# First projection of a two-block transformer kernel: x loaded already transposed on a second DMA queue, row factor moved behind the products, first two weight units run k-outer, small vectors packed

## The chip, the core and the metric

One core of one Trainium2 chip runs the whole program. The metric is the device time in microseconds (us), the median of the runs shown. The engines are TensorE (PE; PEld is its weight load), VectorE (DVE), ScalarE (ACT), GpSimd (POOL) and SyncE (SP, which here only issues DMAs). "SPq" and "ACTq" are the DMA queues of SP and ACT. Each engine runs its own instructions in program order and waits on semaphores.

## What is computed

Two transformer blocks on x of 512 tokens x 1024 features, in float32. Only the start of the first block matters here:

```python
h = rms_norm(x, norm_g)          # x * r * g,  r = rsqrt(mean(x*x) + eps), one r per token
proj = h @ w_in                  # 1024 x 3864
dq, dk, dv, dz, nq, nkv, nz, ng = jnp.split(proj, IN_SPLITS, axis=-1)
dq = rms_norm(dq per head of 64, diff_q_norm_g)     # dk, nq, k_slc, k_win alike
kc, vc = compress(nkv[0], ...), compress(nkv[1], ...)
```

After it come differential attention, the three branches of sparse attention (compressed, selected, window), an output projection, and a second block with a convolution, another attention and a feed-forward net.

## The kernel before, in words

**Split products.** Every float32 projection is made of three reduced-precision products: a weight piece `w_hi` (ACT copies `raw` into it), the rest `w_lo` (POOL subtracts), and likewise `h_hi` (ACT) and `h_lo` (DVE) for the activations. A 128x512 output tile takes 8 k-steps x 3 products = 24 matmuls.

**Units.** Weights come in units of 256 columns (1 MB, two tiles of 128 output features each), in the order dq 0-1, cmp (keys and values to be compressed), dk 0-1, dq 2-3, dk 2-3, nq 0-1, nq 2-3, kd (nsa keys), then the value units. `raw`, `w_hi` and `w_lo` have two slots, so unit n+2 takes the slot of unit n. SP issues the load of a unit when POOL has read the slot's `raw`; ACT splits `w_hi` of the next unit while PE works on this one.

**Plan.** One list of steps (`plan`) is written out beforehand; every engine walks it in the same order and executes its own part of each step. What an engine does for one step therefore stands in front of everything it does for later steps. `later(n, ...)` puts a step n slots on, where a slot is a run of four k-steps (12 matmuls) of PE.

**Head norm.** A tile of kind dq, dk, nq or kd is followed by: squares on ACT into a scratch tile of `L` (L1120 to L1123, read from PSUM), the head's sum of squares as a matmul with a block of ones on PE (`sums`, L1905, one step for the two tiles of a unit, placed after the first 12 matmuls of the next unit or after half of `hidden`), the square root on ACT (L1155, L1156), the reciprocal on DVE (L1460) and the multiplication on POOL (L1040). The tile itself is copied out of PSUM with its gain by DVE (L1401), after ACT's squares.

**cmp tiles.** DVE copies each into `shifted` (L1427, L1428, four copies) and builds `flat` from it (L1436, two additions); `hidden` multiplies that on PE (L2028).

**Start.** SP loads x (four pieces of 512 KB) and then the first unit; ACT's queue has an identity, norm_g and two small tables. ACT and DVE compute the row factor r, DVE scales x by it, PE transposes the scaled x (L1815), ACT and DVE make `h_hi` and `h_lo` from it (L1299, L1762). PE runs 22 idle matmuls first (L2081), and the small matmuls of the bias table (L2085). Twenty small DMAs bring the gain and bias vectors as rows; PE transposes them in one go (L2140), and DVE's `small_arrays` prepares what is derived from them (L1377 to L1393), among it `causal_distance` plus the mask, whose end is signalled as `setup_done` (L1389). The very first squares of a dq tile on ACT wait for `setup_done`.

The three lines that tie the first squares to that setup (two of ACT, one of DVE):

```python
if t.x_in == 1:
    sc.wait_ge(setup_done, 1)
v.tensor_tensor(causal_distance, causal_distance, mask, ALU.add).then_inc(setup_done, 1)
```

Of the kernel before, what the change touches and what calls it, by code (L numbers as in the profile page):

```python
# [9 lines left out]
P = 128  # L10
T = 512
# [21 lines left out]
LAG = 3  # L33
PIECE = 512
# [15 lines left out]
N_SMALL = 20  # L50
# [4 lines left out]
def shape_constants():  # L55
# [10 lines left out]
    steps += [np.full((P, 1), 4.0 ** (h + 1)) for h in range(DIFF_HEADS)]  # L66
    const = np.concatenate([np.eye(P), ones, mask, np.where(ok, 0.0, BIG).reshape(P, -1),
# [44 lines left out]
def build(nc, a, out):  # L112
# [65 lines left out]
    COL_BANK = 5  # L178
# [36 lines left out]
    hi_in_pieces = order[0], *beside_attention, out1_u[0], branch_u[0]  # L215
    ring_in, lo_pieces = [0, 0], Counter()
    for n, u in enumerate(order):
# [8 lines left out]
        ring_in[n % 2] += 16 * (len(u.parts) if u.parts else 1)  # L226
        u.arrived = ring_in[n % 2]
        u.act0 = down_u.index(u) if u.act else None
    next_of = {u.n: order[u.n + 1] if u.n + 1 < len(order) else None for u in order}
# [12 lines left out]
    def evacuated(t):  # L242

        if t.kind in NORM:
            ax_slot(t)
            t.x_in = upto("aux_in")
            t.ve = upto("ve_evac")
# [5 lines left out]
        elif t.kind in ("cmp", "kik", "z", "nz"):  # L253
            t.norms, t.auxes = count["norm_done"], count["aux_done"]
            t.sc = upto("sc_evac") if t.kind in ("z", "nz") else None
            t.ve = upto("ve_evac")
            left[t.bank] = [("ve_evac", t.ve)]
        elif t.kind == "hidden":
# [110 lines left out]
    norms_so_far = [0]  # L369
# [96 lines left out]
    for i in range(NT):  # L466
        emit("row", nth=0, half=1, i=i, res=0)
    left[COL_BANK] = [("col_done", 1)]
    left[4], left[0] = [("rows_done", 1)], [("rows_done", 2)]
    transposed_norm(R_NORM, (1, COL_BANK, 6, 7, 2, 3, 4))  # L470
    first_pieces = [0]

    def small_arrays():

        first_pieces[0] += 1
        if first_pieces[0] != 2:
            return
        col_waits, left[COL_BANK] = left[COL_BANK], [("col_done", 2)]
        emit("small_arrays", waits=col_waits)
# [19 lines left out]
    project(dq_u[:1] + [kv_u] + dk_u[:1], RING4, 4, small_arrays)  # L499
# [194 lines left out]
    with ctx:  # L694
# [10 lines left out]
        lam_in = sb("lam_in", [P, 4, DH])  # L705
# [17 lines left out]
        vec_rows = PT[0:NROWS, 0, 0:P]  # L723
# [20 lines left out]
        dq, dk, nq, dv, kd = (region(2048 * j, 4, T) for j in range(5))  # L744
        vd = region(10240, 2, NT, P)
# [57 lines left out]
        ST_CMN, ST_CSM, ST_TOP, ST_DSS, ST_C2, ST_DC, ST_GNQ, ST_GDQ = 100, 116, 132, 160, 256, 288, 216, 220  # L803
# [28 lines left out]
        def turned_free(t):  # L832

            if t in turned_before:
# [4 lines left out]
        const_in, w0_in = sem("const_in"), sem("w0_in")  # L839
        first_in, small_in, w1_in = sem("first_in"), sem("small_in"), [sem(f"w1_in{j}") for j in range(4)]  # L840
# [8 lines left out]
        col_tr, col_done, setup_done, eps_done = sem("col_tr"), sem("col_done"), sem("setup_done"), sem("eps_done")  # L849
        lam_dot, lam_exp, zero_done = sem("lam_dot"), sem("lam_exp"), sem("zero_done")  # L850

        second_square = sem("second_square")
# [41 lines left out]
                       h_hi_done=h_hi_done, col_done=col_done,  # L894
# [21 lines left out]
        def squares_at(nth, half, i):  # L916

            return max(i, 1) if nth == 0 else NT - 1 + 2 * NT * (nth - 1) + NT * half + i + 1

        def normed_at(nth, i):  # L920

            return (NT + 2) * nth + i + 1

        gains = dict(dq=lambda idx: st[:, ST_GDQ + idx:ST_GDQ + idx + 1], dk=lambda idx: col[:, R_GDK:R_GDK + 1],
                     nq=lambda idx: st[:, ST_GNQ + idx:ST_GNQ + idx + 1], kd=lambda idx: col[:, R_GKS + idx:R_GKS + idx + 1])
# [17 lines left out]
        def _(sp):  # L943
            def load(u):
                if u.n >= 2:
                    wait_free(sp, [(order[u.n - 2].lo_by, order[u.n - 2].lo_end)])
                if u.n == 0:
                    src, half = u.parts[0][0], u.nk // 2
# [6 lines left out]
            def small_loads():  # L955
# [10 lines left out]
                def small(dst, src):  # L966
                    nonlocal n_small
                    sp.dma_start(dst, src).then_inc(small_in, 16)
                    n_small += 1
# [1238 lines left out]
```

## Time and profile before

| what | value |
|---|---|
| median of 3 runs | 1061.03 us (1060.91 to 1061.03) |
| span of the profiled execution, first to last instruction | 1059.3 us |
| PE busy | 1049.8 us (99%) |
| DVE, ACT, POOL busy | 496.7, 455.8, 398.5 us |
| first matmul of the projection starts | 13.37 us |
| PE reaches `hidden` of the compressed keys (144 matmuls and one `sums` later) | 48.58 us |

Read it from PE: almost all of the span is its own work in a row. What another engine does costs time only where PE waits for it. The table gives the one profiled execution; what lies around its span up to the median is 1.7 us.

### The profile page before, as it was taken

The page shows a single profiled execution, that of the slowest core. Times are in us where ns is not written, and L with a number is a line of the kernel's source. Part 1 is how long each engine was busy: PE and PEld are TensorE (multiplying, and loading weights), DVE is VectorE, ACT ScalarE, POOL GpSimd, SP SyncE. Part 2 cuts the span into 40 slices and gives each one's busy share as a digit, 9 for nine tenths or more (in the row PEclk, how much of TensorE's full clock was granted, in tenths as well). Part 3 has the DMA queues.
Part 4 walks back from the last instruction along what each step waited for, and adds up shares of the span by engine and source line. Part 5 has one row for each costly group of instructions (what it writes and reads, how often), then busy time and mean ns, then how long its engine had stood idle before and what let it go on. Part 6 is the DMA issues. An engine that isn't in the chain of part 4 may idle for free.

```text
span 1059.3 us, 14497 instructions
## 1 busy us (share of the span) xinstructions
PE 1049.8 (99%) x5573; PEld 839.1 (79%) x5573; DVE 496.7 (47%) x1047; ACT 455.8 (43%) x794; POOL 398.5 (38%) x300
## 2 busy tenths in 40 slices
PE   9999999999999999999999999999999999999997
PEld 7777897767678876888777888888888888888886
DVE  5754688875752316998587344230000000032444
ACT  6455557676653425233465414342221221233533
POOL 3555520001025334446000255434435354465772
PEclk9999999999999999999999999999999999999999
DMA  9631221201032331332221232323232323323221
GB/s 296 189 117 54 71 80 41 76 16 47 25 120 80 72 118 41 102 98 80 80 80 41 80 103 96 90 79 110 82 116 79 115 83 103 115 80 100 82 97 80
DMA packets 84724, 95.72 MB, mean 90 GB/s; under 512 B 8121, under 2 KB 70930, under 8 KB 84666
## 3 DMA queue, kind: packets, MB, share of 16 engines
q1 hardware_dynamic: 83706, 92.46, 27.9%
q0 software_dynamic: 560, 2.12, 0.6%
q8 instruction: 38, 0.62, 0.2%
q10 hardware_dynamic: 400, 0.35, 0.1%
q14 instruction: 20, 0.16, 0.0%
HBM read 92.80 MB, written 2.12 MB: 90 GB/s over the span
## 4 chain that ended last, share of the span: by engine, by line
PE 97%; DVE 1%; DMA 1%; ACT 1%; issue 0%; ACTq 0%; DVEq 0%
PE bank L1864 59%; PE bank L2177 23%; PE bank L1923 4%; PE bank L1954 3%; PE bank L1995 3%; PE bank L1971 1%; PE bank L2152 1%; PE bank L1815 1%; PE bank L2028 1%; PE bank L1905 1%; DMA PT<-in_onehot 1%; PE bank L1984 0%; PE bank L1947 0%; PE bank L2073 0%; DVE L L1506 0%
## 5 line engine op out<-in xcount | busy, mean ns | idle before, releaser
L1030 POOL TENSOR_TENSOR w_lo<-raw,w_hi 128x512 fp32r<-128x512 f32 (+1 forms) x190 | 266.8, 1434 | 435.1 <-ACT w_hi L1092 422.6
L1864 PE MATMUL bank<-h_hi,w_hi 128*128 128x512 f32 (+1 forms) x560 | 224.4, 401 | 0.3 <-ACT h_hi L1299 0.2
L1864 PE MATMUL bank<-h_hi,w_lo 128*128 128x512 f32 (+1 forms) x560 | 218.7, 390 | 0.0
L1864 PE MATMUL bank<-h_lo,w_hi 128*128 128x512 f32 (+1 forms) x560 | 217.8, 390 | 0.0
L1092 ACT ACTIVATE w_hi<-raw 128x512 fp32r<-128x512 f32 (+3 forms) x94 | 111.3, 1214 | 118.1 <-PE bank L1864 114.5
L1070 POOL TENSOR_TENSOR w_lo<-raw,w_hi 128x512 fp32r<-128x512 f32 x88 | 110.7, 1290 | 133.5 <-ACT w_hi L1337 67.1
L1864 PE MATMUL bank<-w_hi,h_hi 128*128 128x512 f32 (+2 forms) x397 | 145.4, 366 | 0.0
L1864 PE MATMUL bank<-w_hi,h_lo 128*128 128x512 f32 (+2 forms) x397 | 144.5, 364 | 0.0
L1864 PE MATMUL bank<-w_lo,h_hi 128*128 128x512 f32 (+2 forms) x397 | 144.5, 364 | 0.0
L2177 PE MATMUL bank<-h_hi,w_hi 128*128 128x512 f32 x352 | 137.1, 389 | 0.0
L2177 PE MATMUL bank<-h_hi,w_lo 128*128 128x512 f32 x352 | 137.1, 389 | 0.0
L2177 PE MATMUL bank<-h_lo,w_hi 128*128 128x512 f32 x352 | 136.8, 389 | 0.0
L1864 PEld LDWEIGHTS bank<-h_hi,w_hi 128*128 128x128 f32 (+1 forms) x560 | 104.7, 187 | 30.8 <-issue 8.7
L1864 PEld LDWEIGHTS bank<-h_hi,w_lo 128*128 128x128 f32 (+1 forms) x560 | 104.7, 187 | 22.9
L1864 PEld LDWEIGHTS bank<-h_lo,w_hi 128*128 128x128 f32 (+1 forms) x560 | 104.9, 187 | 21.0 <-DVE h_lo L1762 0.4
L1800 DVE TENSOR_TENSOR pool<-bank,L 128x512 f32 (+1 forms) x22 | 15.2, 691 | 215.7 <-PE bank L2177 215.7
L1864 PEld LDWEIGHTS bank<-w_hi,h_hi 128*128 128x128 f32 x397 | 74.8, 188 | 14.5 <-issue 2.1
L1864 PEld LDWEIGHTS bank<-w_hi,h_lo 128*128 128x128 f32 x397 | 74.8, 188 | 11.8
L1864 PEld LDWEIGHTS bank<-w_lo,h_hi 128*128 128x128 f32 x397 | 74.8, 188 | 11.7
L2177 PEld LDWEIGHTS bank<-h_hi,w_hi 128*128 128x128 f32 x352 | 66.1, 188 | 13.9 <-ACT h_hi L1299 0.2
L2177 PEld LDWEIGHTS bank<-h_lo,w_hi 128*128 128x128 f32 x352 | 66.1, 188 | 13.8
L2177 PEld LDWEIGHTS bank<-h_hi,w_lo 128*128 128x128 f32 x352 | 66.1, 188 | 13.7
(211 smaller groups left out, 1240.4 us busy)
## 6 DMA issues: line engine op xcount, KB each, us to landing
raw<-in_w_in SPq DMA_DIRECT2D x29, 1024.0 KB, 5.3
raw<-in_w_ffn_gate SPq DMA_DIRECT2D x11, 1024.0 KB, 5.3
raw<-in_w_ffn_up SPq DMA_DIRECT2D x11, 1024.0 KB, 5.3
raw<-in_w_out SPq DMA_DIRECT2D x8, 1024.0 KB, 5.0
raw<-in_w_ffn_down SPq DMA_DIRECT2D x8, 1024.0 KB, 5.0
raw<-in_w_in SPq DMA_DIRECT2D x8, 512.0 KB, 4.5
pool<-in_cmp_w SPq DMA_DIRECT2D x4, 1024.0 KB, 9.1
raw<-in_w_ffn_down SPq DMA_DIRECT2D x4, 768.0 KB, 4.3
```

The source lines that it names most:

```text
L1030: nc.gpsimd.tensor_tensor(w_lo[:, u.n % 2, cols], raw[:, u.n % 2, cols], w_hi[:, u.n % 2, cols].bitcast(F32), ALU.subtract).then_inc(lo_do ...
L1070: nc.gpsimd.tensor_tensor(w_lo[:, n % 2, cols], raw[:, n % 2, cols], w_hi[:, n % 2, cols].bitcast(F32), ALU.subtract).then_inc(lo_done, 1)
L1092: act_fn(w_hi[:, u.n % 2, cols], raw[:, u.n % 2, cols], ACT.Copy).then_inc(hi_done, 1)
L1800: v.tensor_tensor(x, bank[2 + j][:, :], L[:, j, :], ALU.mult).then_inc(act_done, 1)
L1815: return nc.tensor.transpose(bank[t.bank][:, P * i:P * i + P], zs[:, i, P * t.idx:P * t.idx + P], ident)
L1864: ins = mm(bank[t.bank][0:t.m, 0:u.width if u.token else T], stationary, moving, start=first and n == 0, stop=last and n == len(products) ...
L1905: ins = mm(bank[banks[half]][o:o + DH, :], ones[rows, rows], scratch(t)[rows, :], start=True, stop=True)
L1923: ins = mm(bank[S_BANKS[c]][:, columns(job, p)], q, k, start=True, stop=True)
L1954: ins = nc.tensor.transpose(dst[:, o:o + P], L[:, (job.r + c) % LRING, o:o + P], ident)
L1971: ins = mm(O[:, P * p:P * p + P], turned(job.t)[:, o:o + P], dv[:, j, P * g:P * g + P], start=j == 0, stop=j == i)
L1995: ins = mm(O[DH * half:DH * half + DH, P * i:P * i + P], x, turned(job.t + half)[:, o:o + P], start=dsa and j == 0, stop=j == i and (dsa o ...
L2177: ins = mm(bank[2 * j + m][:, :], w[:, k, P * m:P * m + P], x[:, k, :], start=n == 0, stop=n == len(products) - 1)
```

## The change

- **x arrives transposed.** The host lays x out as `x_t` (feature by token); ACT's queue loads `cols` (all small vectors, already as columns) and then x_t in 8 pieces of 256 KB, then the two tables. SP's queue loads the first two units in 8 pieces of 256 KB, then the constants, the lambda vectors and `distance`. PE's transposes, their PSUM tiles and the 20 small DMAs are gone. x in its old layout (needed for the residual) is loaded after unit 6.
- **Row factor behind the products.** `h_hi` and `h_lo` are made from x_t times norm_g only. ACT squares x_t, DVE adds the squares up, PE multiplies by ones (`ss`), ACT takes the root and DVE the reciprocal, into `rbc` (r for every token, on all partitions). Each output tile of this block is multiplied by `rbc` when DVE takes it out of PSUM (dv and vd tiles: by a column on ACT).
- **Head norm.** DVE now takes the tile out first (times `rbc`); ACT squares the copy in SBUF; for dk and kd tiles ACT then also multiplies it by the gain in place. q gains are folded into the k gains.
- **nz and z tiles.** DVE takes the tile out, ACT makes tanh of the copy, and DVE finishes it one slot later (`z_finish`): one more DVE instruction per tile, 8 tiles.
- **k-outer head.** The first two units run together: for each k, 4 tiles x 3 products, with waits on each piece. The third unit's `w_hi` is split in four pieces as the head frees them.
- **Places.** `small_arrays` and the bias-table matmuls stand behind the head, in the third unit.

The pieces of the diff, in this order: the plan; ACT's head; ACT's squares of a tile; DVE taking tiles out (norm tiles, then cmp tiles); the loads on ACT's queue.

```diff
-    project(dq_u[:1] + [kv_u] + dk_u[:1], RING4, 4, small_arrays)
+    emit("head")
+    emit("split", u=order[2], of=order[1])
+    for o in range(0, PIECE * len(head_part), PIECE):
+        emit("high_piece", u=order[2], o=o)
+    for t in head_tiles[:2]:
+        evacuated(t)
+    emit("high_piece", u=order[2], o=PIECE * len(head_part))
+    for t in head_tiles[2:]:
+        evacuated(t)
+    for u in head_units:
+        follow(u)
+    project(dk_u[:1], RING4, 4, small_arrays)
...
+            def head():
+                for q in range(ND // 2):
+                    for k in (2 * q, 2 * q + 1):
+                        sc.wait_ge(xt_in[k], 16)
...
+                        act_fn(h_hi[:, k, :], x_t[:, k, :], ACT.Copy, scale=col[:, R_NORM + k:R_NORM + k + 1]).then_inc(h_hi_done, 1)
+                        for j in range(2) if k % 2 == 0 else ():
...
+                            act_fn(w_hi[:, j, cols], raw[:, j, cols], ACT.Copy).then_inc(hi_done, 1)
...
+                        act_fn(square_rows[:, k % 2, :], x_t[:, k, :], ACT.Square).then_inc(sq_done, 1)
+                sc.wait_ge(ss_mm, 1)
+                act_fn(rbc[:, :], bank[4][:, :], ACT.Sqrt, scale=1.0 / D, bias=eps).then_inc(r_root, 1)
...
-                sc.wait_ge(tile_done, t.done)
-                if kind in NORM + AUX_COPY:
+                if kind in NORM:
                     if t.x_in == 1:
                         sc.wait_ge(setup_done, 1)
+                    sc.wait_ge(ve_evac, t.ve)
...
+                    if t.squared:
+                        ins.then_inc(row_squares, 1)
+                        sc.wait_ge(row_squares, t.squared)
+                        ins = act_fn(x, x, ACT.Copy, scale=gains[kind](idx))
...
                 if kind in NORM:
-                    ve.wait_ge(aux_in, t.x_in)
+                    ve.wait_ge(tile_done, t.done)
...
+                    if kind in ("dq", "nq"):
+                        v.scalar_tensor_tensor(dests[kind][:, idx, :], src[:, :], steps_at(kind, idx), rbc[:, :],
+                                               ALU.mult, ALU.mult).then_inc(ve_evac, 1)
+                    else:
+                        v.tensor_tensor(dests[kind][:, idx, :], src[:, :], rbc[:, :], ALU.mult).then_inc(ve_evac, 1)
...
-                        v.tensor_copy(shifted[0:DH, idx, kv, :], src[half, :])
+                        v.tensor_tensor(shifted[0:DH, idx, kv, :], src[half, :], rbc[half, :], ALU.mult)
...
+            sc.dma_start(col[:, :], a["cols"]).then_inc(cols_in, 16)
+            for k in range(ND):
+                sc.dma_start(x_t[:, k, :], a["x_t"][:, k, :]).then_inc(xt_in[k], 16)
```

How instructions now stand, at three places.

On DVE, at the setup. `L1389` before and `L1456` after are the addition that signals `setup_done`; L1401 takes dq tiles out of PSUM before, L1516 ends the second cmp tile after. Before:

```order
L1381 TENSOR_SCALAR st<-const,col 128x4 x2
L1383 TENSOR_SCALAR col<-col 128x16
L1384 TENSOR_SCALAR col<-col 128x1
L1386 ISA lam_in,st<-lam_in 128x64
L1386 ISA st 128x1
L1386 ISA lam_in,st<-lam_in 128x64
L1386 ISA st 128x1
L1389 TENSOR_TENSOR pool<-pool,const 128x512
L1391 TENSOR_TENSOR st<-st 128x1
L1393 TENSOR_SCALAR st<-st 128x1
L1401 TENSOR_SCALAR pool<-bank,st 128x512 x2
```

After:

```order
L1516 TENSOR_TENSOR zs<-zs,col 128x496 x2
L1448 TENSOR_SCALAR col<-col 128x1
L1449 TENSOR_SCALAR col<-col 128x3
L1450 TENSOR_SCALAR col<-col 128x16
L1451 TENSOR_SCALAR col<-col 128x1
L1453 ISA pool,st<-pool 128x64
L1453 ISA st 128x1
L1453 ISA pool,st<-pool 128x64
L1453 ISA st 128x1
L1456 TENSOR_TENSOR pool<-pool,const 128x512
L1458 TENSOR_TENSOR st<-st 128x1
```

The setup stood ahead of every tile that DVE takes out; now it stands behind two dq tiles and both cmp tiles.

On ACT, from the last work of the first activations to the first squares (L1123, L1120, L1121 before; L1168, L1166 after) and the weight splits (L1092 before; L1130 after). Before:

```order
L1299 ACTIVATE h_hi<-bank,col 128x512 [waits tile_done] x2
L1092 ACTIVATE w_hi<-raw 128x2048 [waits raw_in1]
L1322 ACT_TABLE_LOAD
L1322 ACTIVATE st<-st 128x2 [waits lam_dot]
L1123 ACTIVATE L<-bank 128x512 [waits setup_done,tile_done]
L1120 ACTIVATE L<-bank 64x512 [waits tile_done]
L1121 ACTIVATE L<-bank 64x512
L1092 ACTIVATE w_hi<-raw 128x2048 [waits tile_done,raw_in0]
```

After:

```order
L1119 ACTIVATE rbc<-bank,st 128x512 [waits ss_mm]
L1120 ACTIVATE st<-bank,st 128x4
L1130 ACTIVATE w_hi<-raw 128x512 [waits part_done,raw_in0] x3
L1168 ACTIVATE L<-pool 128x512 [waits ve_evac,setup_done]
L1166 ACTIVATE L<-pool 64x512 [waits ve_evac]
L1166 ACTIVATE L<-pool 64x512
L1130 ACTIVATE w_hi<-raw 128x512 [waits tile_done,raw_in0]
L1130 ACTIVATE w_hi<-raw 128x2048 [waits tile_done,raw_in1]
```

The first squares wait for `setup_done` as before and now for DVE's copy too; the last piece of the third unit's `w_hi` and the whole fourth unit stand behind them.

On DVE, at the reciprocals (L1460 before, L1540 after) and the tiles taken out around them (L1401 before, L1476 and L1473 after); L1731 and L1804 copy `hidden`. Before:

```order
L1460 RECIPROCAL L<-L 128x512 x2
L1427 COPY zs<-bank 64x512
L1428 COPY zs<-bank 64x511
L1427 COPY zs<-bank 64x512
L1428 COPY zs<-bank 64x511
L1436 TENSOR_TENSOR zs<-zs,col 128x496 x2
L1401 TENSOR_SCALAR pool<-bank,col 128x512 x2
L1731 COPY pool<-bank 62x128 x2
```

After:

```order
L1464 TENSOR_SCALAR L<-bank 8x512
L1476 TENSOR_TENSOR pool<-bank,rbc 128x512
L1540 RECIPROCAL L<-L 128x512 x2
L1476 TENSOR_TENSOR pool<-bank,rbc 128x512
L1804 COPY pool<-bank 62x128 x2
L1473 SCALAR_TENSOR_TENSOR pool<-bank,const,rbc 128x512 x2
```

The second dk tile is taken out behind the two reciprocals of the dq tiles both times; but ACT's squares of that tile come ahead of it before, and from it after.

## Rows read from the trace of the kernel before

**Rows 1.** Page, part 1: busy time, share of the span, instructions of each engine.

```profile
PE 1049.8 (99%) x5573; PEld 839.1 (79%) x5573; DVE 496.7 (47%) x1047; ACT 455.8 (43%) x794; POOL 398.5 (38%) x300
```

**Rows 2.** Whom PE waited for, whole span: total us, times, longest us.

```profile
PE bank L2081 <- POOL vc L1042: 1.0, 1, 1.0
PE bank L2085 <- DMA PT<-in_onehot: 0.4, 1, 0.4
```

**Rows 3.** Chain that ended last, in order of time: start us, us, what.

```profile
28.28 1.02 PE bank L1905 x8
29.30 19.28 PE bank L1864 x84
48.58 1.90 PE bank L2028 x32
125.39 5.95 PE bank L1864 x48
```

**Rows 4.** Timeline of the start: start us, us, engine, line, op, out<-in, count [idle before].

```profile
0.75 1.82 SPq L985 DMA_DIRECT2D xres<-in_x  x4
1.01 3.86 PE L2081 MATMUL bank<-vc 128*128 128x128 f32 x20 [1.01 <-POOL vc L1042]
5.32 2.94 PE L2081 MATMUL bank<-vc 128*128 128x128 f32 x24
8.71 1.24 PE L2085 MATMUL bank<-PT,relb 32*8 32x128 f32 x4 [0.44 <-DMA PT<-in_onehot]
10.98 1.16 ACT L1085 ACTIVATE w_hi<-raw 128x512 fp32r<-128x512 f32 x2
13.37 1.04 PE L1864 MATMUL bank<-h_hi,w_hi 128*128 128x512 f32 x2 [0.21 <-ACT h_hi L1299]
17.76 1.41 DVE L1762 SCALAR_TENSOR_TENSOR h_lo<-bank,col,h_hi 128x512 fp32r<-128x512 f32 x2 [0.27 <-ACT h_hi L1299]
19.36 0.36 DVE L1381 TENSOR_SCALAR st<-const,col 128x4 f32<-128x4 f32 x2
20.06 0.68 DVE L1389 TENSOR_TENSOR pool<-pool,const 128x512 f32<-128x512 f32 x1
```

**Rows 5.** Timeline of DVE from 26 us, same columns.

```profile
26.83 0.75 DVE L1401 TENSOR_SCALAR pool<-bank,st 128x512 f32<-128x512 f32 x1 [0.96 <-ACT L L1121]
32.99 0.68 DVE L1428 COPY zs<-bank 64x511 f32<-64x511 f32 x1
35.13 1.94 DVE L1436 TENSOR_TENSOR zs<-zs,col 128x496 f32<-128x496 f32 x2
36.99 6.55 DVE L1460 RECIPROCAL L<-L 128x512 f32<-128x512 f32 x2
46.40 3.71 DVE L1436 TENSOR_TENSOR zs<-zs,col 128x496 f32<-128x496 f32 x2
```

**Rows 6.** Timeline of POOL: four pieces without, then with, DVE's additions beside them.

```profile
29.61 5.04 POOL L1030 TENSOR_TENSOR w_lo<-raw,w_hi 128x512 fp32r<-128x512 f32 x4 [1.37 <-ACT w_hi L1092]
44.87 6.32 POOL L1030 TENSOR_TENSOR w_lo<-raw,w_hi 128x512 fp32r<-128x512 f32 x4
```

**Rows 7.** Timeline of ACT: squares, table load, root.

```profile
27.61 1.91 ACT L1092 ACTIVATE w_hi<-raw 128x2048 fp32r<-128x2048 f32 x1 [0.82 <-DMA raw<-in_w_in]
29.54 1.28 ACT L1155 ACT_TABLE_LOAD   x1
30.84 0.69 ACT L1155 ACTIVATE L<-bank,st 64x512 f32<-64x512 f32 x1
49.22 0.59 ACT L1121 ACTIVATE L<-bank 64x512 f32<-64x512 f32 x1
```

**Rows 8.** Stages: us, busy PE PEld DVE ACT POOL (count), PEclk, DMA share, GB/s.

```profile
5.00:10.00 5.00, 4.39 (x30) 3.27 (x31) 3.71 (x10) 3.52 (x8) 0.00 (x0) 1.00 1.03 363
250.00:304.00 54.00, 52.91 (x455) 37.62 (x453) 37.40 (x133) 38.03 (x103) 5.05 (x4) 1.00 0.07 21
1056.00:1059.30 3.30, 0.00 (x0) 0.00 (x0) 0.15 (x1) 0.21 (x1) 0.00 (x0) 0.50 0.53 210
```

More of the change, by code:

```diff
@@ L33 @@
 LAG = 3
+HEAD_LO = 8
 PIECE = 512
@@ L497, in hidden @@
         later(1, turn_hidden)
-    project(dq_u[:1] + [kv_u] + dk_u[:1], RING4, 4, small_arrays)
+    head_units = order[:2]
+    head_tiles = head_units[0].tiles + head_units[1].tiles
+    for t in head_tiles:
+        t.bank, t.waits = take(RING4)
+        t.done = upto("tile_done")
+    for k in range(ND):
+        h_hi_at[R_NORM, k] = ("h_hi_done", upto("h_hi_done"))
+        h_lo_at[R_NORM, k] = ("h_lo_done", upto("h_lo_done"))
+    head_part = [upto("part_done") for _ in range(ND // 2 - 1)]
+    for u in head_units:
+        u.used = ("tile_done", u.tiles[-1].done)
+    left[4] = left[5] = [("r_root", 2)]
+    emit("head")
[7 more added lines that the diff above has]
+        evacuated(t)
+    for u in head_units:
+        follow(u)
+    project(dk_u[:1], RING4, 4, small_arrays)
     hidden(0)
@@ L1370, in _, with head @@
             v.memset(eps, EPS).then_inc(eps_done, 1)
[L1371 to L1372 removed]
+            def head():
+                for q in range(ND // 2):
+                    for k in (2 * q, 2 * q + 1):
+                        ve.wait_ge(h_hi_done, k + 1)
+                        v.scalar_tensor_tensor(h_lo[:, k, :], x_t[:, k, :], col[:, R_NORM + k:R_NORM + k + 1],
+                                               h_hi[:, k, :].bitcast(F32), ALU.mult, ALU.subtract).then_inc(h_lo_done, 1)
+                    for k in (2 * q, 2 * q + 1):
+                        if k == 0:
+                            continue
+                        ve.wait_ge(sq_done, k + 1)
+                        if k > 1:
+                            ve.wait_ge(sq_added, k - 1)
+                        v.tensor_tensor(square_sum, square_rows[:, 0, :] if k == 1 else square_sum, square_rows[:, k % 2, :],
+                                        ALU.add).then_inc(sq_added, 1)
+                ve.wait_ge(r_root, 1)
+                v.reciprocal(rbc[:, :], rbc[:, :]).then_inc(r_done, 1)
+                ve.wait_ge(r_root, 2)
+                chain(v.reciprocal(st[:, ST_RR:ST_RR + NT], st[:, ST_RS:ST_RS + NT]))
+                v.tensor_scalar(st[:, ST_SS:ST_SS + NT], st[:, ST_RR:ST_RR + NT], 0.5, None, ALU.mult).then_inc(r_done, 1)
+                ve.wait_ge(r_done, 2)
+                ve.wait_ge(const_in, 16)
```

365 lines of the change are left out of this document (202 added, 163 removed).

## The prediction

> **What bounds the kernel now.** I read the busy shares first: PE is busy for 99% of the span, the other engines for less than half [rows 1]. Then whom PE waited for: apart from its first wait for GpSimd's memset, no wait is longer than half a microsecond [rows 2]. Then the chain that ended last: from 29.30 us, PE does 84 matmuls in 19.28 us, 0.2295 us each, and goes on to `hidden` at 48.58 without a gap [rows 3]. So once the projection runs, time is PE's work plus any wait that a change puts into it. What lies ahead is the start: the first product is at 13.37 us [rows 4]. A change can win there, and must not make PE wait afterwards. The trace's span is 1059.3 us, the median 1061.03; I sum on the span and add the same 1.7 us.
>
> **The start.** ACT's queue issues 11 DMAs before ACT's first work. SP's four x loads took 1.82 us to issue [rows 4], so I take 11 x 0.455 = 5.0 us, from 0.76 to 5.8 us; then a table load of 1.28 [rows 7] and a one-element root 0.2 (an estimate), one `h_hi` and one `w_hi` piece at 0.58 each [rows 4]: the first product at about 8.5 us. The data are no later: some 0.8 MB must have landed, and the queues moved 363 GB/s between 5 and 10 us [rows 8]. That nearly all x bytes ride on ACT's queue beside SP's the trace does not show; bounds 7.0 and 13.4 us, and I take 8.5, since the issue times are the nearer rows. Gain 4.9 us.
>
> **The head.** 96 matmuls x 0.2295 = 22.0 us. First weight rests are late for the second unit: 0.4. The `ss` products are plain float32 as the bias-table products are, 640 columns in 1.24 us [rows 4]; 512 of them cost 0.99, and four tiny ones I put at 0.1 each: 1.4 us. DVE now has two-input subtractions and additions from SBUF beside POOL's subtractions. Where that happened before, DVE's pair of additions took 3.71 instead of 1.94 us [rows 5], and POOL's four pieces 6.32 instead of 5.04 [rows 6]; so they mostly take turns. Per quarter of the head that is 2 x 1.26 us of POOL and 4 x 0.7 of DVE, 5.3 us against PE's 5.5, and `ss` needs the last quarter's additions when PE only begins that quarter. Bounds 0 (no overlap) and 4 us (strict turns); I take 2.5. Head ends at 8.5 + 0.4 + 22.0 + 1.4 + 2.5 = 34.8, and with the next 12 matmuls (2.75) PE stands at `sums` of the dq tiles at 37.5.
>
> The Trainium skill ("SBUF — State Buffer", section "SBUF: two separate sides") calls the port pair of VectorE and GpSimd an exclusive lock, taken also by a VectorE instruction with two SBUF inputs. The trace agrees for the most part: 3.71 + 6.32 us overlapped where 1.94 + 5.04 alone would give 6.98 in turns and 6.32 passed [rows 5, 6]. By the rule to the letter the sum is 1.5 us higher.
>
> **The first wait: setup behind the tiles.** `sums` needs ACT's squares of both dq tiles. The first square waits for `setup_done`, and DVE reaches it only after everything in front. From the end of `ss`: root on ACT 0.69 [rows 7], reciprocal of 128x512 at 6.55 / 2 = 3.28 [rows 5], two small instructions 0.35 (an estimate from the setup's), two dq tiles at 0.75, two cmp tiles at 4 x 0.68 + 1.94 = 4.7 each [rows 5], the setup from 19.36 to 20.74 = 1.4 [rows 4], and ACT's squares 3 x 0.59 [rows 7]: 0.7 + 3.3 + 0.35 + 1.5 + 9.4 + 1.4 + 1.8 = 18.4 us. In that time PE has only 24 + 12 matmuls, 8.25 us. PE waits 10.2 us, to 47.7. Behind the squares on ACT stand the last piece of the third unit's `w_hi` and the fourth unit; those land while PE does `sums` (1.02) [rows 3], the bias-table products (1.24) and six more matmuls, so I cost them at nothing; without that cover, 1 us. Then 36 matmuls, 8.3: PE is at `hidden` at 58.2 where it was at 48.58: **+9.6 us**, the earlier start included.
>
> **The later waits: reciprocals in front of the tile.** Before, ACT squared a tile straight from PSUM, and DVE took it out whenever it came to it, 6.55 us of reciprocals or not. Now squares follow DVE, and in the order of instructions the second tile of four units stands behind two reciprocals of the pair before, which themselves wait for the roots, which on ACT stand behind the squares of the same unit's first tile. From the end of that first tile: DVE 0.7, square and gain copy 1.2, first tile's root 1.38, reciprocals 6.55, DVE 0.7, squares and gain copy 1.8 = 12.3 us; the dk unit after the setup has a table load (1.28) too, the nq unit has the table load but no gain copies (13.1). PE meanwhile has 24 matmuls (5.5) and then half a `hidden` (1.9), or 12 matmuls (2.75), or, for kd, the compressed scores (1.9, an estimate from `hidden`) and 24 narrow matmuls (5.95 / 48 each, 2.9) [rows 3]. Waits: dk 0-1 13.6 - 7.4 = 6.2; dk 2-3 12.3 - 7.4 = 4.9; nq 2-3 13.1 - 8.2 = 4.9; kd 12.3 - 10.3 = 2.0. Sum **18.0 us**. The other pairs come with 0.5 us to spare.
>
> The Trainium skill ("ScalarE: Activation LUTs", section "What ACT_TABLE_LOAD costs") adds a drain of 1.38 us to each load's 1.28. Here the load begins at 29.54, 0.02 after the split ended, and the root follows 0.02 after it [rows 7], so the trace shows no drain. By the page, two waits would be 1.4 longer each, 2.8 in all.
>
> **Restarts.** After idling, PE is slow at first: its first 20 idle matmuls took 3.86 us, the next 24 took 2.94 [rows 4], 0.193 against 0.123 each, 1.4 us lost. At the end of the kernel the granted clock is down to 0.50, the lower of 2.4 and 1.2 GHz, some 3 us after PE's last matmul [rows 8]. Four of the five waits are longer than that: 4 x 1.4 = **5.6 us**; bounds 0 and 8.
>
> **The rest.** nz and z tiles give DVE 8 more instructions of about 0.7 us while it is busy 37.4 of 54 us [rows 8], and free PSUM one hand-over earlier: nothing; if DVE's slack is short where it counts, up to 2 us. The later x load (2 MB) has most of a unit's time free on the queues: nothing. All other units, the second block and the end are unchanged.
>
> **Sum.** 9.6 + 18.0 + 5.6 = 33.2 us; 1059.3 + 33.2 + 1.7 = 1094.2, say **1094 us**.
>
> **Rivals.**
> - *Faster: the squares arrive in time.* If DVE's way from `ss` to the squares took less than PE's 8.25 us and not 18.4, and the reciprocals found room, no wait would come: 9.6 - 10.2 = -0.6, and without DVE and POOL taking turns -3.1: 1058 us. Against it: the reciprocal and the two cmp tiles alone are 12.7 us [rows 5]. Chance 0.05.
> - *Only the setup wait.* If DVE is free when the second tiles end, the four later waits go: 1061 + 9.6 + 1.4 = 1072. For it: a long first wait lets DVE catch up; against it: the roots are released by PE's own `sums`, so reciprocals move with it. Chance 0.08.
> - *x late on ACT's queue.* If the transposed pieces share the engines badly and the first product comes no sooner than 13.4, everything moves by 4.9: 1099. For it: the table on ACT's queue let PE wait in the trace [rows 2], while SP's loads ran. Chance 0.12.
> - *As forecast.* Chance 0.75.
>
> **Numbers.** About 0.2% (2 us) is what a measurement of this kernel can tell from no change. The forecast's own terms: start -1.5 to +2.5, turns -2.5 to +1.5, restarts -5.6 to +2.4, later waits -3 to +4, attention 0 to +2, so 1081 to 1107; the late x lies inside, the two others are left out with 0.13. Slower: 0.94; same: 0.02; faster: 0.04.
>
> **What would show it.** Right: first product near 8.5 us; PE idle about 10 us before the first `sums`, released by ACT's squares, these by DVE's setup addition; four more gaps of 2 to 6 us before `sums`, each with two DVE reciprocals in front; PE clock below 1 after them; nothing new after 160 us. Wrong: PE without gaps between 35 and 160 us; a gap of another releaser (a DMA, POOL's weight rests); or new waits in attention. If DVE's tiles times `rbc` take much longer than plain copies, the first wait grows by that, eight times over.

## The result, and the profile after

The changed kernel takes 1108.41 us (median of four runs, 1107.68 to 1108.78) against 1060.97 us for the kernel before on the same chip: a ratio of 1.0445, 95% interval 1.0431 to 1.0460. Slower was forecast, by 33 us; it is 47, and the time lies 14 us above the forecast of 1094 and 1.4 us above the end of its range. The profiled execution has a span of 1106.8 us where the kernel before had 1059.3.

The page of the changed kernel: span, busy time by engine, and the granted clock of PE in 40 slices of 27.7 us.

```profile
span 1106.8 us, 14461 instructions
PE 1062.1 (96%) x5541; PEld 844.2 (76%) x5541; DVE 509.8 (46%) x1051; ACT 465.2 (42%) x808; POOL 399.2 (36%) x301
PEclk9789988999999999999999999999999999999999
```

PE's share fell from 99% [rows 1] to 96%, and it has 12 us more busy time although it has less to do: a part of its work ran at a lower clock. Whom PE waited for in the changed kernel (total us, times, longest us):

```profile
PE bank L1977 <- ACT L L1166: 15.4, 2, 10.2
PE bank L2180 <- ACT w_hi L1113: 2.5, 1, 2.5
PE bank L1977 <- ACT pool L1172: 12.1, 2, 6.7
PE bank L1977 <- ACT zs L1172: 2.3, 1, 2.3
PE bank L1995 <- DVE st L1586: 1.8, 3, 1.4
PE bank L2043 <- ACT PT L1286: 0.9, 1, 0.9
```

Before, no wait but the first was over half a microsecond [rows 2]. Now five waits stand ahead of `sums` (L1977), each for ACT's squares or gain copies: 10.2, 6.7, 5.4, 5.2 and 2.3, together 29.8 us. The chain that ended last names what stood in front of them (start us, us, what; lines left out between):

```profile
46.45 0.61 DVE pool L1456
...
49.06 1.98 PE bank L1977 x8
51.05 2.23 PE bank L2239 x4
53.27 4.54 PE bank L1936 x12
...
62.67 6.57 DVE L L1540 x2
69.24 0.56 DVE pool L1476
...
71.89 1.98 PE bank L1977 x8
73.87 3.48 PE bank L2100 x32
...
166.31 1.99 PE bank L1977 x8
168.29 7.87 PE bank L1936 x48
```

In front of the first `sums` is DVE's setup addition (L1456), which ends at 47.06 us; in front of the second are two reciprocals, 6.57 us together (L1540), and then the second dk tile (L1476). Three more pieces of this form lead to the `sums` at 109.17, 147.10 and 166.31 us. And each time PE comes back slowly: `sums` takes 1.98 us where it took 1.02, 32 products of `hidden` 3.48 where they took 1.90, twelve projection products 4.54 where twelve at 0.2295 make 2.75, 48 narrow ones 7.87 where they took 5.95 [rows 3]. The stages show why (us, busy us of PE, PEld, DVE, ACT and POOL with counts, granted clock, DMA share, GB/s):

```profile
38.50:49.00 10.50, 0.35 (x2) 0.00 (x0) 8.42 (x18) 1.87 (x3) 0.00 (x0) 0.71 0.00 1
49.00:51.10 2.10, 2.04 (x9) 0.40 (x10) 0.00 (x0) 2.08 (x3) 1.27 (x1) 0.50 0.00 0
71.80:74.00 2.20, 2.11 (x10) 0.50 (x12) 0.00 (x0) 0.10 (x2) 0.00 (x0) 0.50 0.00 0
166.30:169.00 2.70, 2.69 (x11) 1.09 (x12) 0.09 (x1) 2.66 (x3) 1.64 (x2) 0.50 0.00 0
```

Behind each wait PE runs at a granted clock of 0.50, the lower of its two levels, for some microseconds.

The account, by PE's own marks in the two traces: the five waits are 29.8 us, and the slow stretches behind them, each against the same products at full speed before, lost 3.7 + 2.5 + 2.7 + 2.7 + 2.9 = 14.5 us. Attention starts at 193.48 us where it started at 148.66: +44.8, so that the earlier start and the new head (PE is done with it, and at its first `sums`, at 38.86 us) together come to half a microsecond. Attention adds 2.6 more (a product of the sparse part that was at 208.77 is now at 256.17, +47.4), and from there to the end nothing changes.

### The profile page after: what moved, and what is told of

Same layout as the page of the kernel before. It is cut to its first block, busy times and chain, and to the rows that moved or that the text cites. A ratio compares the mean times of both kernels' runs of the same rounds, so it can differ in the third digit from the quotient of the medians.

```text
span 1106.8 us, 14461 instructions
## 1 busy us (share of the span) xinstructions
PE 1062.1 (96%) x5541; PEld 844.2 (76%) x5541; DVE 509.8 (46%) x1051; ACT 465.2 (42%) x808; POOL 399.2 (36%) x301
## 4 chain that ended last, share of the span: by engine, by line
PE 87%; DVE 7%; ACT 3%; issue 2%; ACTq 1%; DVEq 0%
PE bank L1936 51%; PE bank L2277 22%; PE bank L1995 4%; PE bank L2026 3%; PE bank L2067 3%; DVE L L1540 2%; PE bank L1977 1%; PE bank L2252 1%; DVE pool L1434 1%; PE bank L2043 1%; PE bank L2100 1%; ACT L L1166 1%; DVE L L1586 0%; PE bank L1888 0%; ACTq L1324 0%
## 5 line engine op out<-in xcount | busy, mean ns | idle before, releaser
L1039 POOL TENSOR_TENSOR w_lo<-raw,w_hi 128x512 fp32r<-128x512 f32 (+1 forms) x182 | 255.0, 1432 | 458.6 <-ACT w_hi L1130 458.6
L1936 PE MATMUL bank<-h_hi,w_hi 128*128 128x512 f32 (+1 forms) x528 | 213.5, 404 | 0.6 <-DVE pool L1473 0.6
L1936 PE MATMUL bank<-h_hi,w_lo 128*128 128x512 f32 (+1 forms) x528 | 207.1, 392 | 0.0
L1936 PE MATMUL bank<-h_lo,w_hi 128*128 128x512 f32 (+1 forms) x528 | 206.3, 392 | 0.0
L1130 ACT ACTIVATE w_hi<-raw 128x512 fp32r<-128x512 f32 (+3 forms) x96 | 109.6, 1174 | 111.1 <-PE bank L1936 110.4
L1936 PEld LDWEIGHTS bank<-h_hi,w_hi 128*128 128x128 f32 (+1 forms) x528 | 99.6, 189 | 32.0 <-issue 8.0
L1936 PEld LDWEIGHTS bank<-h_hi,w_lo 128*128 128x128 f32 (+1 forms) x528 | 99.5, 188 | 22.0
L1936 PEld LDWEIGHTS bank<-h_lo,w_hi 128*128 128x128 f32 (+1 forms) x528 | 99.8, 189 | 19.8 <-DVE h_lo L1835 0.2
```

The costliest lines, as they stand in the source:

```text
L1039: nc.gpsimd.tensor_tensor(w_lo[:, u.n % 2, cols], raw[:, u.n % 2, cols], w_hi[:, u.n % 2, cols].bitcast(F32), ALU.subtract).then_inc(lo_do ...
L1130: act_fn(w_hi[:, u.n % 2, cols], raw[:, u.n % 2, cols], ACT.Copy).then_inc(hi_done, 1)
L1936: ins = mm(bank[t.bank][0:t.m, 0:u.width if u.token else T], stationary, moving, start=first and n == 0, stop=last and n == len(products) ...
```

## Experiments

All are made from the changed kernel. Each is compared with the kernel before, run on the same chip, at 1061.0 to 1061.2 us. Line numbers in their rows are each kernel's own.

**One (e1_setup_early): the setup addition early.** It alone moves, into the stretch in which DVE waits for the root.

```diff
@@ VectorE, head()
+                ve.wait_ge(small_in, 16 * N_SMALL)
+                ve.wait_ge(const_in, 16)
+                v.tensor_tensor(causal_distance, causal_distance, mask, ALU.add).then_inc(setup_done, 1)
                 ve.wait_ge(r_root, 1)
                 v.reciprocal(rbc[:, :], rbc[:, :]).then_inc(r_done, 1)
@@ VectorE, small_arrays()
-                v.tensor_tensor(causal_distance, causal_distance, mask, ALU.add).then_inc(setup_done, 1)
```

> One instruction moves: VectorE's setup addition (the mask into the distance array, 0.68 us at 46.37 in the changed kernel) goes ahead of its wait for the root, where VectorE stands idle from 27.7 to 30.4 us. ScalarE's first squares wait for it, and TensorE's first sums for them. Theory A (the prediction's steps, each wait stands alone): the first wait of 10.2 us and the slow stretch behind it (3.7 us) go and nothing follows: 1108.4 - 13.9 = 1094.5 us. Theory B (VectorE's queue is the limit, and a wait removed at one place comes back at the next): VectorE still has the four compression evacuations up to 45.7 us and the small arrays after them in front of dk's first tile, so that this tile is evacuated at some 50 us instead of 57.8; the wait at dk's first sums grows from 6.7 to some 12 us, and the gain is some 8 us: 1100.5 us.

Measured: 1100.75 us (ratio 1.0373, 1.0356 to 1.0390), theory B within 0.3 us. PE's waits:

```profile
PE bank L1979 <- ACT pool L1172: 17.3, 2, 11.9
PE bank L1979 <- ACT L L1166: 5.1, 1, 5.1
```

The wait of 10.2 us is gone: the first `sums` starts at 38.7 us. But the next one grew from 6.7 to 11.9. DVE still had the compression tiles and the small arrays to do, and the dk tiles stood behind these. So the first wait is caused by the place of the setup addition, as the prediction said, but taking it away is worth 7.7 us and not 13.9: most of the rest comes back at the next `sums`, which waits for the same DVE queue.

**Two (e2_squares_first): squares ahead of the evacuation.** With the setup early, the squares of dq, dk, nq and kd come from PSUM again, and DVE's evacuation follows them.

```diff
@@ ScalarE, evacuate(t), kind in NORM
-                    sc.wait_ge(ve_evac, t.ve)
+                    sc.wait_ge(tile_done, t.done)
                     wait_free(sc, t.ax_waits)
-                    x = dests[kind][:, idx, :]
...
+                        ins = act_fn(scratch(t), src, ACT.Square)
@@ VectorE, evacuate(t), kind in NORM
-                    ve.wait_ge(tile_done, t.done)
+                    ve.wait_ge(aux_in, t.x_in)
...
+                    v.tensor_scalar(dests[kind][:, idx, :], src[:, :], gain, None, ALU.mult).then_inc(ve_evac, 1)
```

> Setup addition early as in e1, and for the tiles dq, dk, nq and kd the squares go back to ScalarE reading the accumulator itself, with VectorE's evacuation (gain only, no row factor) behind them. The head norm divides the row factor out again, so what is computed stays the same up to the epsilon under the root. Theory A (the 29.8 us of waits before the five sums are the chain evacuation on VectorE, then square, then sums): all five go, with the 14.5 us of slow stretches behind them: 1108.4 - 44.3 = 1064 us; some us more if a bank now comes free late, up to 1070. Theory B (the loss lies in the new head and its loads, or in the row factor's work elsewhere): at least half of the loss of 47 us stays: 1085 us or more.

Measured: 1068.68 us (1.0072, 1.0055 to 1.0089). This reordering, with the early setup, takes back 39.7 of the 47.4 us. In its trace four of the five waits and all the slow stretches are gone. The edit does three things at once for these tiles: the squares come first, the row factor is left off, and ACT's gain copies of dk and kd go; what each of them is worth was not tried apart. One wait is left, and its chain says whose it is:

```profile
PE bank L1968 <- ACT L L1162: 2.5, 1, 2.5
```

```profile
45.32 0.70 DVE zs L1499
...
46.98 1.00 DVE zs L1507
...
48.69 0.20 ACT st L1363
...
49.40 1.28 ACT L1207
...
53.50 0.59 ACT L L1161
...
54.75 1.09 PE bank L1968 x8
```

The compression tiles (L1499, L1507) hold the lambda products on DVE; ACT's exponential (L1363) waits for these, and the roots (L1207) and dk's second squares (L1161) stand behind it.

**Three (e3_fill_waits): the waits filled.** PE does idle products in front of the five waits.

```diff
@@ TensorE, sums(pair, banks, waits)
-                pe.wait_ge(aux_in, pair[1].x_in)
                 wait_free(pe, waits)
                 if pair[0].aux == 1:
                     pe.wait_ge(const_in, 16)
+                for _ in range({('dq', 0): 40, ('dk', 0): 26, ('dk', 2): 20, ('nq', 2): 20, ('kd', 0): 8}.get((pair[0].kind, pair[0].idx), 0)):
+                    mm(bank[banks[0]][:, 0:P], ones, ones, start=True, stop=True)
+                pe.wait_ge(aux_in, pair[1].x_in)
```

> Ahead of the five long waits TensorE gets idle products (128 columns of ones into the bank that the sums overwrite; 40, 26, 20, 20 and 8 of them at some 0.245 us each, a little less than each wait). The waits themselves end when they did. Theory A (the slow products after each wait come from TensorE's idling): granted clock 1.00 behind each sum, the 14.5 us of slow stretches go: 1108.4 - 14.5 = 1094 us, the waits stay as long as they were. Theory B (the clock falls there for another reason, such as the sums' own 64-row products): 1108 us or more, with clock 0.50 behind the sums as before.

Measured: 1095.75 us (1.0325, 1.0308 to 1.0342), 12.7 us under the changed kernel, with work added and nothing taken away. The idle products ahead of the first wait (two instructions each) with the `sums` behind them, and the stages behind the first three waits:

```profile
39.12 9.09 PE L1973 MATMUL bank<-const 128*128 128x128 f32 x80
49.59 1.09 PE L1979 MATMUL bank<-L,const 64*64 64x512 f32 x8 [1.38 <-ACT L L1166]
```

```profile
52.20:57.00 4.80, 4.80 (x16) 3.88 (x17) 2.69 (x5) 1.29 (x2) 4.80 (x4) 0.73 0.93 292
71.00:74.00 3.00, 3.00 (x43) 2.27 (x36) 0.50 (x2) 2.34 (x4) 0.00 (x0) 1.00 0.00 0
107.00:112.00 5.00, 5.00 (x41) 3.90 (x38) 3.67 (x3) 4.91 (x6) 0.79 (x1) 1.00 0.00 0
```

`sums` is at 1.09 us again and the clock at 1.00 behind four of the waits. Only behind the first it still fell, at about 51 us, after 1.4 us of idling, while PE did `sums` and the four bias-table products; that stretch cost 1.8 us. The traced execution was the slowest of the four (1096.83 us, the others 1095.6 to 1095.8 at a higher mean clock), so whether the others had this stretch, and what parts the 14.5 us expected from the 12.7 measured, isn't shown. With PE kept busy the slow stretches go behind four waits of five: they come of idling, and they are the price put on each of these waits beyond its length.

**Four (e5_short_reciprocals): short reciprocals.** DVE's reciprocals of the head norms work on a quarter of the columns.

```diff
@@ VectorE, finish(t), kind in NORM
-                    v.reciprocal(r, r).then_inc(recip_done, 1)
+                    v.reciprocal(r[:, 0:P], r[:, 0:P]).then_inc(recip_done, 1)
```

> VectorE's reciprocals of the head norms work on 128 of the 512 columns, so some 0.85 instead of 3.3 us each; the rest of those norm factors is left out. Theory A (the later waits are the second tile of a unit behind two reciprocals on VectorE): the wait at dk's first sums falls from 6.7 to about 1.9 us, those of 5.4, 5.2 and 2.3 us go, and three or four slow stretches of 2.5 to 2.9 us with them; the first wait of 10.2 us stays: 1108.4 - 17.8 - 8.3 = 1082 us. Theory B (those waits are ScalarE's own chain of squares, roots and table loads): within 3 us of 1108 us.

Measured: 1083.67 us (1.0219, 1.0202 to 1.0236), close to the 1082 of theory A. PE's waits:

```profile
PE bank L1977 <- ACT L L1166: 11.2, 2, 10.2
PE bank L1977 <- ACT pool L1172: 3.6, 2, 2.5
```

The first wait stands as it was; the four later ones shrank from 19.6 us to 4.6 (2.5, 1.1, 1.0 and nothing), and the slow stretches behind them are gone. The reciprocals in front of the second tile are what made them.

**Five (e7_gates_as_before): the gates as before, in the changed kernel.** The z and nz tiles go back to tanh from PSUM and one DVE instruction.

```diff
@@ ScalarE, evacuate(t), kind in ("z", "nz")
-                    sc.wait_ge(ve_evac, t.ve)
-                    if t.z > 2:
-                        sc.wait_ge(z_done, t.z - 2)
+                    sc.wait_ge(tile_done, t.done)
...
+                    act_fn(mix(idx + (4 if kind == "nz" else 0)), src, ACT.Tanh, scale=0.5).then_inc(sc_evac, 1)
@@ VectorE, evacuate(t), kind in ("z", "nz")
-                    v.tensor_tensor(x, src[:, :], rbc[:, :], ALU.mult).then_inc(ve_evac, 1)
+                    ve.wait_ge(sc_evac, t.sc)
+                    v.scalar_tensor_tensor(x, x, 1.0, src[:, :], ALU.add, ALU.mult).then_inc(ve_evac, 1)
```

> One part of the change undone in the changed kernel: the z and nz tiles (the output gates beside attention) are taken as before, ScalarE's tanh from the accumulator and one VectorE instruction behind it, without the row factor, which is left out there. Theory A (the 2.6 us that attention lost come from ScalarE's tanh having to stand behind VectorE's evacuation, which is itself queued behind VectorE's attention work): 1108.4 - 2.6 = 1105.8 us, with the TensorE waits of 1.4 and 0.9 us at the passage from the differential heads to the sparse ones gone. Theory B (that loss comes from the shift of attention against the weight loads or from the row factor elsewhere): 1108.4 us, waits unchanged.

Measured: 1103.30 us (1.0401, 1.0386 to 1.0415), 5.1 under the changed kernel where 2.6 was expected. The profiled span is 1103.7, 3.1 shorter, and in it the mark of the sparse part (the product named above) moves from 256.17 to 253.14; the waits of 1.4 and 0.9 us have gone. What the other 2 us of the medians are, this run doesn't tell; its times scatter from 1102.5 to 1106.1. The next three kernels, where no slow stretch disturbs, measure the same part better.

**Six to eight (e8_small_early, e89_tanh_later, e87_small_early_gates): small arrays early; then the gates.** To experiment two, the first adds the move of DVE's remaining small arrays to its idle stretch:

```diff
@@ VectorE, head()
                 v.tensor_tensor(causal_distance, causal_distance, mask, ALU.add).then_inc(setup_done, 1)
+                v.tensor_scalar(col[:, R_GDK:R_GDK + 1], col[:, R_GDK:R_GDK + 1], col[:, R_GDQ:R_GDQ + 1], None, ALU.mult)
...
+                                           accum_out=st[:, ST_LAM + j:ST_LAM + j + 1]).then_inc(lam_dot, 1)
                 ve.wait_ge(r_root, 1)
```

> e2_squares_first with all of VectorE's small arrays (gains, lambda products) moved ahead of its wait for the root, where it is idle. In e2 one wait was left, 2.5 us at dk's first sums, where ScalarE's exponential of lambda stood waiting for the products behind VectorE's compression evacuations, and dk's squares behind it. Theory A (that wait is this order): 1068.7 - 2.5 = 1066.2 us, no wait over 0.5 us at any of the sums. Theory B (ScalarE is short of time there): the wait stays, 1068.5 us.

Measured: 1064.67 us (1.0033, 1.0021 to 1.0045): 4.0 us less than experiment two, and no wait over half a microsecond at any `sums`. Theory A, with 1.5 us more than its 2.5.

On top of it, ACT's tanh one step later in its order (and DVE's finish one more behind):

```diff
@@ planner, evacuated(t), kind in ("z", "nz")
-            t.sc = upto("sc_evac")
...
-            later(1, lambda: emit("z_finish", t=t))
+            def tanh():
+                t.sc = upto("sc_evac")
+                emit("z_tanh", t=t)
+
+            later(1, tanh)
+            later(2, lambda: emit("z_finish", t=t))
```

> e8 with ScalarE's tanh of each z and nz tile put one step later in its order, and VectorE's finishing instruction one more behind that; nothing is left out. Theory A (attention's loss is ScalarE standing at the tanh until VectorE's evacuation of the tile): 1066.2 - 2.6 = 1063.6 us. Theory B (VectorE's additional instruction is the cost, 0.6 us at each tile in a stretch that VectorE paces): 1066 us, no change.

Measured: 1063.36 us (1.0020, 1.0011 to 1.0029). That is 1.3 us under experiment six, between the 2.6 of theory A and the nothing of theory B; the time itself comes to theory A's 1063.6 only because experiment six was 1.5 us under what was expected of it. And, instead of that, the gates as in experiment five:

> e8 with the z and nz tiles as before (as in e7; their row factor is left out). What is left of the change is then the new head and the row factor in the compression and value tiles. Theory A (waits, slow stretches and attention are the whole loss, and the start is worth what it gained): about 1061 to 1063.6 us. Theory B (the new head alone costs time): above 1064 us.

Measured: 1062.25 us (1.0010, 1.0001 to 1.0019), theory A; what is left of the change, without the gates' row factor, costs 1.1 us. The waits of PE inside attention, in these three in turn:

```profile
PE bank L1987 <- DVE st L1578: 1.8, 3, 1.4
PE bank L2035 <- ACT PT L1278: 0.9, 1, 0.9
```

```profile
PE bank L1994 <- DVE st L1585: 0.4, 2, 0.2
PE bank L2042 <- ACT PT L1279: 0.9, 1, 0.9
```

```profile
PE bank L1979 <- DVE st L1575: 0.4, 2, 0.2
```

In the kernel before no wait of PE behind its first was over half a microsecond [rows 2]. So the row factor's way through DVE costs attention 2.4 us: 1.3 because ACT stands at the tanh while DVE has attention's work ahead of the tile (the later place takes that away, the 1.4 us wait with it), and 1.1 that go only with the old form of the gates, and the wait of 0.9 us with them. That these 1.1 are DVE's additional instruction is argued: the old form also has the tanh from PSUM and leaves the row factor out.

**Nine (e10_split_issue): the start's loads shared out.** From experiment seven: ACT's queue keeps the columns and two pieces of x; SP's takes six pieces and the bias tables.

```diff
@@ SyncE, head loads
                     sp.dma_start(slot(raw, j, u)[:, ks, :], u.parts[0][0][:, ks, :]).then_inc(head_in[2 * q + j], 16)
+                for k in range(max(2 * q + 2, 2), min(2 * q + 4, ND)):
+                    sp.dma_start(x_t[:, k, :], a["x_t"][:, k, :]).then_inc(xt_in[k], 16)
@@ ScalarE
-            for k in range(ND):
+            for k in range(2):
                 sc.dma_start(x_t[:, k, :], a["x_t"][:, k, :]).then_inc(xt_in[k], 16)
-            sc.dma_start(relb[:, :], a["rel_bias_2"]).then_inc(table_in, 16)
-            sc.dma_start(onehot, a["onehot"]).then_inc(table_in, 16)
```

> e89 with the start's loads shared out: ScalarE's queue issues only the columns and the first two pieces of x, SyncE's queue the other six between the weights, and the two tables of the bias after them. ScalarE's issues ahead of its table load then end near 2.2 us instead of 7.1 to 7.8, and the first product can come at about 7 instead of 9.9 to 10.6 us. Theory A (the head is TensorE's own time, so what the start gains stays to the end): 1063.4 - 3 = 1060.4 us, at or under the kernel before. Theory B (the loads' arrival or VectorE's head work, 1.4 to 3.5 us for two instructions, then hold TensorE): a loss of under 1 us against e89, 1062.5 us or more.

Measured: 1060.71 us (0.9996, 0.9987 to 1.0005), theory A (expected 1060.4); no difference from the kernel before. ACT's first rows, in the changed kernel and then here, here with PE's first product:

```profile
1.23 4.62 ACTq L1324 DMA_DIRECT2D zs<-in_x_t  x8
7.07 1.28 ACT L1328 ACT_TABLE_LOAD   x1 [7.07 <-issue]
8.37 0.20 ACT L1328 ACTIVATE st<-st 128x1 f32<-128x1 f32 x1
8.48 0.71 ACT L1109 ACTIVATE h_hi<-zs,col 128x512 fp32r<-128x512 f32 x1
```

```profile
2.27 1.28 ACT L1323 ACT_TABLE_LOAD   x1 [2.27 <-issue]
5.77 0.72 ACT L1117 ACTIVATE h_hi<-zs,col 128x512 fp32r<-128x512 f32 x1 [2.00 <-DMA zs<-in_x_t]
7.16 1.17 PE L2181 MATMUL bank<-h_hi,w_hi 128*128 128x512 f32 x4 [0.36 <-ACT w_hi L1121]
```

The first product comes at 7.16 us, where it came at 9.85 in the changed kernel and at 10.60 in the trace of experiment seven; by the medians 2.65 of this stay to the end. What held the start was ACT issuing eleven DMAs ahead of its own first work: in the changed kernel its first split, at 8.48, waits for no data, and here it waits 2.0 us for them.

**Ten (e12_pool_short): GpSimd out of the way.** In the changed kernel's head POOL's pieces are a sixteenth as wide.

```diff
@@ GpSimd, head()
-                        nc.gpsimd.tensor_tensor(w_lo[:, j, cols], raw[:, j, cols], w_hi[:, j, cols].bitcast(F32), ALU.subtract)\
+                        part = slice(PIECE * q, PIECE * q + 32)
+                        nc.gpsimd.tensor_tensor(w_lo[:, j, part], raw[:, j, part], w_hi[:, j, part].bitcast(F32), ALU.subtract)\
```

> In the new head GpSimd's low parts work on 32 of 512 columns, and TensorE's products of low weights take the high ones instead (the low weights of the first two units are left out). Theory A (VectorE's head instructions with two operands in SBUF take turns with GpSimd): all pairs of h_lo and of additions take 1.4 to 1.5 us, as the pair at 20.1 us does in the changed kernel while GpSimd is idle, and not 3.5; the squares' sum is ready earlier by several us than 27.8. Theory B (their length comes from waiting for ScalarE or from the form of the instruction): 2.4 to 3.5 us as before. The whole time moves by less than 3 us either way, since TensorE waited only 2 us in the head.

Measured: 1106.82 us, a single run, so the argument goes by its trace alone. DVE in the changed kernel, with POOL busy and (at 20.10) with POOL idle, then in this one:

```profile
13.28 3.49 DVE L1426 SCALAR_TENSOR_TENSOR h_lo<-zs,col,h_hi 128x512 fp32r<-128x512 f32 x2
16.70 3.48 DVE L1434 TENSOR_TENSOR pool<-pool 128x512 f32<-128x512 f32 x2
20.10 1.40 DVE L1426 SCALAR_TENSOR_TENSOR h_lo<-zs,col,h_hi 128x512 fp32r<-128x512 f32 x2
```

```profile
13.13 0.75 DVE L1427 SCALAR_TENSOR_TENSOR h_lo<-zs,col,h_hi 128x512 fp32r<-128x512 f32 x1
15.46 1.48 DVE L1435 TENSOR_TENSOR pool<-pool 128x512 f32<-128x512 f32 x2
```

Theory A: beside POOL's subtractions a pair takes 2.5 times as long. But the first `sums` comes only 1.0 us earlier (48.09 us), from a first product 0.6 us later; so DVE and POOL taking turns cost the head 1.6 us.

**Eleven (e13_chain_short): the chain behind the head shortened.** On experiment nine, the sum of squares stands seven products later on PE, and DVE's short chain on the row roots goes behind the first evacuations.

```diff
@@ TensorE, head()
-                    if k == ND - 2:
+                        if k == ND - 2 and (n, p) == (2, 1):
@@ VectorE, head()
-                chain(v.reciprocal(st[:, ST_RR:ST_RR + NT], st[:, ST_RS:ST_RS + NT]))
...
+                ve.wait_ge(r_done, 1)
@@ VectorE, small_arrays()
+                chain(v.reciprocal(st[:, ST_RR:ST_RR + NT], st[:, ST_RS:ST_RS + NT]))
```

> e10 with the chain behind the head shortened: TensorE's sum of squares stands seven products later in the head (so that the 1.3 us in which it waited for VectorE's last addition fill with products), and VectorE's reciprocal of the four columns of row roots with its doubling (1.3 us ahead of the first evacuations in e10) goes behind those evacuations. Theory A (the chain sum of squares, root, reciprocal, evacuation sets the start of the third unit): that unit starts some 1.0 to 1.3 us earlier and this stays to the end: 1060.7 - 1.2 = 1059.5 us, under the kernel before by some 0.15%. Theory B (VectorE's later queue, or the weights' arrival for the third unit, takes it back): 1060.7 us.

Measured: 1060.02 us (0.9990, 0.9981 to 0.9999): 0.7 us under experiment nine where 1.2 was expected, and 1.0 us under the kernel before, less than the 0.2% that can be called a gain. The third unit waits 1.0 us for DVE's first tile where it waited 0.6, so a part went into that wait. It is the fastest version found.

## Why the prediction was right, and where it was wrong

**The direction and the chain of causes were right.** PE's bound, the first wait behind the setup addition (10.2 us forecast, 10.2 measured; experiment one) and the later waits behind two reciprocals (18.0 forecast, 19.6 measured; experiment four) are there, and so are the signs listed for a right forecast, with two misses: the first product, and attention, where new waits of 1.4 and 0.9 us stand that were listed as a sign of being wrong. That the first wait agrees to a tenth is in part luck: DVE's two small instructions took 1.2 us where 0.35 was put, and PE lost about as much ahead of the wait, 0.6 of it at its bank. The rivals of a faster kernel and of the setup wait alone fell with the five waits in the trace, that of x late on ACT's queue with the first product at 9.85 us.

**The step that failed is the term for the restarts: 5.6 us, with a bound of 8, measured 14.5.** Two things were wrong in it. Its size was taken from the kernel's first idle products, which lost 1.4 us [rows 4]; after a wait the whole run of products at clock 0.50 counts, and it lost 2.5 to 3.7 us. And I let the wait of 2 us for kd go free, where its 2.3 us cost 2.9 behind it. Two stages of the kernel before, its first 5 us and the last ones of PE, show that neither number had the support that I gave it:

```profile
0.00:5.00 5.00, 3.86 (x20) 3.67 (x20) 0.06 (x1) 1.61 (x3) 0.41 (x5) 1.00 0.63 191
1053.00:1056.00 3.00, 0.16 (x2) 0.00 (x0) 2.65 (x8) 2.47 (x9) 0.00 (x0) 0.86 0.71 294
```

The first idle products ran at a granted clock of 1.00 by the trace, so what slowed them isn't shown to be what slows PE behind a wait. And at the end, where PE is busy for only the first 0.16 us of these 3, the mean clock is down to 0.86 before the 1056 us from which I read the 0.50 [rows 8], so that row gave no ground for calling a shorter wait free. How long PE stays at 0.50 once it works again, no row of the kernel before shows. Experiment three took some 12.7 us back, against these 14.5, although the data came no sooner. With 14.5 in place of 5.6 the sum would have been 1103.1 us.

**Attention was put at nothing, with a bound of 2, and cost 2.6** in the trace, 2.4 by experiments six and eight. The cover that the prediction named, DVE's 37.4 busy of 54 us [rows 8], is a mean over the stretch; at the passage from the differential to the sparse heads DVE's queue had no room, and ACT stood at the tanh behind it.

**Smaller terms.** The later waits were 1.6 us longer than forecast, each by 0.3 to 0.5. The first product came at 9.85 and not at 8.5. The eleven issues took 6.3 us where 5.0 was forecast, since those that carry x took 0.58 each and the two tables' 0.57 on average, not SP's 0.455 [rows 4]; what follows took as long as forecast. The head's loss by turns was 1.6 where 2.5 was taken (and in this 1.6 is the half microsecond for the second unit's weight rests); the products of `ss` took 1.9 and not 1.4, and the third unit waited 0.6 for its bank. These cancel, by luck: the head took the 29.0 us that were forecast, and PE came to the first wait 1.4 us later, all of it from the start. The sum of differences, 8.9 + 2.6 + 1.6 + 1.4 = 14.5, against 47.5 - 33.2 = 14.3 in the spans.

**What the prediction's sum does not say**, though its second rival touches it, is that the waits are not separate costs. Taking the first away gave 7.7 of 13.9 us back (experiment one), since the same DVE queue then held the next `sums`.

The Trainium skill ("SBUF — State Buffer", section "SBUF: two separate sides") was cited for VectorE and GpSimd taking turns; experiment ten agrees, with 1.4 us for a pair of DVE's instructions alone and 3.5 beside POOL. The drain that the Trainium skill puts around a table load ("ScalarE: Activation LUTs", section "What ACT_TABLE_LOAD costs") isn't seen here either: the load at 7.07 us ends at 8.35, and the next ACT instruction begins at 8.37, as the rows under experiment nine show.

## What to carry to other kernels

Where PE is the bound, price a new wait as its length and then, where the clock falls, the products that follow at half the clock: here 2.5 to 3.7 us more for each of five waits, and nothing more in the traces of two other kernels with a wait of 2.5 us. Before moving an evacuation ahead of the work that others wait for, look at what stands in front of it in its engine's order: here two reciprocals or a setup addition stood in front of 29.8 us of waits, and an early setup addition with the squares back ahead of the evacuation recovered 40 of 47 us. A factor that a later norm divides out again, up to the epsilon under its root, need not be multiplied in on the way at all.

## What the runs showed of the hardware

- The clock's fall doesn't follow from the length of a wait alone. In the changed kernel a wait of 2.3 us ahead of the fifth `sums` was followed by clock 0.50; waits of 2.5 us in experiments two and four were not, as these two stages of experiment four show (during the wait, and behind it). What tells them apart was not tried. Two of the four executions of experiment two were 1.1 to 1.7 us longer than the other two, at a mean clock of 0.997 and 0.995 against 0.999, so the clock may have fallen in those; they have no trace.

```profile
65.40:67.90 2.50, 0.02 (x2) 0.00 (x0) 0.42 (x1) 1.98 (x3) 1.23 (x1) 1.00 0.00 0
67.90:72.00 4.10, 4.07 (x45) 2.91 (x46) 0.99 (x3) 2.84 (x5) 0.00 (x0) 1.00 0.00 0
```

- DVE's instructions with two SBUF operands and POOL's subtractions slow each other: 0.70 us for one of DVE's alone, 1.74 beside POOL (experiment ten); four pieces of POOL 5.04 us alone, 6.32 beside DVE [rows 6].
- A DMA issue on ACT's queue took 0.45 to 0.68 us of ACT's time in the changed kernel; three of them instead of eleven ahead of its first instruction brought the first product from 9.85 to 7.16 us (experiment nine), and then it was the data that came last.
